# Key normalisation steps moved in VectorE's order, rho and one product on GpSimd, an earlier load of tk, and clears on GpSimd, in a decoder layer with two recurrent mixers

## The reference, cut to what matters

```python
kk = kk / jnp.maximum(jnp.linalg.norm(kk, axis=-1, keepdims=True), 1e-12)
k_mod = heads(kf * (1.0 + (a - 1.0) * rw_k_a))
# S_t = S_{t-1} diag(w_t) + (S_{t-1}(-kk_t)) (kk_t*a_t)^T + v_t k_t^T ; y_t = S_t r_t
y = _rwkv7_scan(r_h, w_h, k_mod, v_h, kk, kk * a_h)
y = (y - mu) * lax.rsqrt(var + GN_EPS) * gn_w + gn_b      # per head
y = y + jnp.sum(r_h * k_mod * rw_r_k, axis=-1, keepdims=True) * v_h
hm = _mlstm_chunkwise(mh(q2), mh(k2), mh(v2), i_pre + ml_i_b, f_pre + ml_f_b)
hm = (hm - mu) * lax.rsqrt(var + ML_NORM_EPS)             # per head
```

## Time and profile before

| what | us |
|---|---|
| median of 3 runs (lowest, highest) | 2936.3 (2933.69, 2939.88) |
| profiled execution, its own time | 2934.89 |
| its span | 2933.0 |
| TensorE busy | 2840.8 (97%) |
| VectorE, GpSimd, ScalarE busy | 1292.5, 1226.8, 581.7 |

### The profile page before, as it was taken

The page is one execution under the profiler, slowest core; times in us unless marked ns, Lnnn a source line. Parts: engine busy times, 40 slices in busy tenths (PEclk is TensorE's granted clock), DMA queues, the critical chain, the costliest instruction groups (busy, mean ns, idle before and its releaser), DMA issues.

```text
span 2933.0 us, 38258 instructions
## 1 busy us (share of the span) xinstructions
PE 2840.8 (97%) x14892; PEld 2379.6 (81%) x14892; DVE 1292.5 (44%) x1207; ACT 581.7 (20%) x908; POOL 1226.8 (42%) x651
## 2 busy tenths in 40 slices
PE   7999999999999999989999999999999999999996
PEld 5888888888888888868888888887888888888885
DVE  5331432244556524127888876532444422331344
ACT  3100110012100112125656641112311100100011
POOL 3334433443444356644556454332133443343341
PEclk9999999999999999999999999999999999999998
DMA  3111111112322234332112214320011111111112
GB/s 131 48 50 50 44 49 50 51 41 95 111 90 100 100 101 152 117 103 55 49 34 54 48 51 129 108 79 29 8 49 51 46 48 50 50 44 49 51 41 74
DMA packets 99115, 196.61 MB, mean 67 GB/s; under 512 B 14288, under 2 KB 56400, under 8 KB 98792
## 3 DMA queue, kind: packets, MB, share of 16 engines
q1 hardware_dynamic: 79072, 138.07, 16.0%
q10 hardware_dynamic: 19976, 57.59, 5.2%
HBM read 160.93 MB, written 34.67 MB: 67 GB/s over the span
## 4 chain that ended last, share of the span: by engine, by line
PE 90%; DVE 6%; issue 2%; ACT 1%; POOL 1%; DMA 1%; DVEq 0%; ACTq 0%; SPq 0%; POOLq 0%
PE G L655 26%; PE G L657 26%; PE G L656 26%; PE G L884 4%; PE G L1053 1%; PE G L787 1%; PE G L1076 1%; PE G L973 1%; PE G L781 0%; DVE ylo L1959 0%; DVE kk L1717 0%; DVE beta L1793 0%; DMA tk<-rows_d 0%; PE G L721 0%; DVE Am L1847 0%
## 5 line engine op out<-in xcount | busy, mean ns | idle before, releaser
L614 POOL TENSOR_TENSOR whi<-raw,zero 128x1024 fp32r<-128x1024 f32 (+1 forms) x213 | 398.9, 1873 | 1409.8 <-PE G L657 1406.3
L655 PE MATMUL G<-hhi,whi 128*128 128x512 f32 x2288 | 893.4, 390 | 17.8 <-DVE hlo L1538 17.8
L657 PE MATMUL G<-hhi,wlo 128*128 128x512 f32 x2288 | 890.9, 389 | 0.0
L656 PE MATMUL G<-hlo,whi 128*128 128x512 f32 x2288 | 890.9, 389 | 0.0
L617 POOL TENSOR_TENSOR wlo<-raw,whi 128x1024 fp32r<-128x1024 f32 (+1 forms) x213 | 517.3, 2428 | 16.7
L655 PEld LDWEIGHTS G<-hhi,whi 128*128 128x128 f32 x2288 | 430.0, 188 | 109.3 <-issue 15.3
L657 PEld LDWEIGHTS G<-hhi,wlo 128*128 128x128 f32 x2288 | 429.9, 188 | 89.7
L656 PEld LDWEIGHTS G<-hlo,whi 128*128 128x128 f32 x2288 | 430.1, 188 | 89.3 <-issue 0.7
L655 PE MATMUL G<-ahi,whi 128*128 128x512 f32 x960 | 374.5, 390 | 2.7 <-DVEq L436 2.7
L656 PE MATMUL G<-alo,whi 128*128 128x512 f32 x960 | 374.2, 390 | 0.0
L657 PE MATMUL G<-ahi,wlo 128*128 128x512 f32 x960 | 374.1, 390 | 0.0
(11 more groups left out here) (328 smaller groups left out, 3183.8 us busy)
## 6 DMA issues: line engine op xcount, KB each, us to landing
raw<-in_wg SPq DMA_DIRECT2D x44, 512.0 KB, 3.5
raw<-in_wu SPq DMA_DIRECT2D x44, 512.0 KB, 3.5
raw<-in_wd SPq DMA_DIRECT2D x32, 512.0 KB, 3.5
raw<-in_ml_in SPq DMA_DIRECT2D x16, 512.0 KB, 3.6
zml_d<-po ACTq DMA_DIRECT2D x16, 512.0 KB, 2.6
gates_d<-po ACTq DMA_DIRECT2D x16, 512.0 KB, 2.7
zm<-zml_d SPq DMA_DIRECT2D x8, 1024.0 KB, 5.8
sg<-gates_d ACTq DMA_DIRECT2D x16, 512.0 KB, 5.0
```

The source lines that it names most:

```text
L614: nc.gpsimd.tensor_tensor(hi, raw[:, k, 0:w], zero[:].to_broadcast([P, w]), ALU.add).then_inc(hi_made, 1)
L655: nc.tensor.matmul(dst, wh, hi, start=start, stop=False)
L656: nc.tensor.matmul(dst, wh, lo, start=False, stop=False)
L657: return nc.tensor.matmul(dst, wl, hi, start=False, stop=stop)
```

## The change

It has eight parts, all in the mixers' stage.

1. `key_root(i + 1, 0)` moves from behind level 6 to between its two updates, into the place of the product Ys*yrs. `key_root(i, 1)` moves from the end of pass i - 1 into pass i behind "cc", where `key_root(i, 2)` and `kk` go as well, ahead of gsig, ga, gu and kmod (in pass 0 they stay behind kmod).
2. The product Ys*yrs ("y1") goes from VectorE to GpSimd, as the first of its output instructions.
3. GpSimd's rho also waits for `bv` of VectorE.
4. TensorE's transposes of kap now come ahead of the mean, those of beta behind it; ScalarE copies ktok ahead of btok.
5. `tk` of segment 0 is loaded by ScalarE's queue in the projection of the gates, not by SyncE behind the barrier.
6. Am is filled in `first_keys`; Bm, Mv and Mu are cleared by GpSimd in pass 0.
7. The mLSTM's statistics (`mve`, `mmv`, lines 1889 to 1894) go from level 2 to behind the first update of level 3; `output_norm(0)` goes from level 3 to level 4.
8. FINAL_SEQ and the lists of names follow (of them the diff shows one).

```diff
--- before.py
+++ after.py
@@ -115,4 +115,4 @@
 B_ACT = ["Un", "Y0", "Y1", "lnv", "rsv"]
-B_DVE = ["dS", "S", "yc", "ve", "g1", "g2", "g3", "y1"]
-B_POOL = ["bvb", "ysq", "y2", "y3", "y4"]
+B_DVE = ["dS", "S", "yc", "ve", "g1", "g2", "g3"]
+B_POOL = ["bvb", "ysq", "y1", "y2", "y3", "y4"]
 M_PE = ["kT", "vT", "S", "num", "dC", "yT"]
@@ -481,4 +482,5 @@
                 sp.dma_start(ab[:], rows_d[0:2, :, cols].unsqueeze(0).to_broadcast([P, 2, MH, SEG])).then_inc(rows_in, 16)
-                sp.dma_start(tk[:], rows_d[2:4, :, cols].rearrange("k h t -> t k h"),
-                             allow_slow_non_contiguous=True).then_inc(rows_in, 16)
+                if back:
+                    sp.dma_start(tk[:], rows_d[2:4, :, cols].rearrange("k h t -> t k h"),
+                                 allow_slow_non_contiguous=True).then_inc(rows_in, 16)
                 sp.wait_ge(*m_dve.at("y1", i - 1))
@@ -550,3 +552,5 @@
 
-                pool.wait_ge(*b_dve.at("y1", j))
+                pool.wait_ge(*b_dve.at("g3", j))
+                tt(Ys[:], Ys[:], yrs[:], ALU.mult).then_inc(*B.sig("y1"))
+                pool.wait_ge(*B.at("y1", j))
                 tt(Ys[:], Ys[:], vbc("rw_gn_w", SEG), ALU.mult).then_inc(*B.sig("y2"))
@@ -559,2 +563,5 @@
                 tt(bvb[:], bv[:], vbc("rw_gn_b", SEG), ALU.add).then_inc(*B.sig("bvb"))
+            if front and not back:
+                for m in (Bm, Mv, Mu):
+                    nc.gpsimd.memset(m[:], 0.0)
             if front:
@@ -569,2 +576,3 @@
                 pool.wait_ge(*b_pe.at("Y", j))
+                pool.wait_ge(*f_dve.at("bv", i))
                 tt(rho[:], zs[:, 0:4, :], Pp[:, :, 1:DEC], ALU.mult).then_inc(*F.sig("rho"))
@@ -856,4 +864,2 @@
                 turn(g1[:, 1, :], zs[:, 8:12, :]).then_inc(*F.sig("vT"))
-                pe.wait_ge(*f_dve.at("bv", i))
-                turn(g0[:, 1, :], beta).then_inc(*F.sig("bT"))
                 pe.wait_ge(*f_pool.at("kap", i))
@@ -864,2 +870,4 @@
             if front:
+                pe.wait_ge(*f_dve.at("bv", i))
+                turn(g0[:, 1, :], beta).then_inc(*F.sig("bT"))
                 pe.wait_ge(*f_act.at("ktok", i))
@@ -1261,2 +1269,5 @@
                 if n == RC - 1:
+                    act.wait_ge(rows_out, 4 * 16)
+                    act.dma_start(tk[:], rows_d[2:4, :, 0:SEG].rearrange("k h t -> t k h"),
+                                  allow_slow_non_contiguous=True).then_inc(rows_in, 16)
                     act.wait_ge(x_in, 4 * 16)
@@ -1334,4 +1345,4 @@
             if front:
-                for name, dst, src in (("a", atok, g0[:, 0, :]), ("v", vtok, g1[:, 1, :]), ("b", btok, g0[:, 1, :]),
-                                       ("k", ktok, g1[:, 0, :])):
+                for name, dst, src in (("a", atok, g0[:, 0, :]), ("v", vtok, g1[:, 1, :]), ("k", ktok, g1[:, 0, :]),
+                                       ("b", btok, g0[:, 1, :])):
                     act.wait_ge(*f_pe.at(f"{name}T", i))
@@ -1720,2 +1731,3 @@
             step(nc.vector.memset(mvx[:], 1.0))
+            step(nc.vector.tensor_copy(Am[:], con(C_ID).unsqueeze(1).to_broadcast([P, NH, P])))
             key_sums(i)
@@ -1726,4 +1738,3 @@
                 dve.wait_ge(kv_out[r], (RC + RC // 2 + 1) * 16)
-            step(nc.vector.tensor_copy(Am[:], con(C_ID).unsqueeze(1).to_broadcast([P, NH, P])))
-            for m in (Bm, Mv, Mu, St, CN):
+            for m in (St, CN):
                 step(nc.vector.memset(m[:], 0.0))
@@ -1757,8 +1768,5 @@
                     tt(w, w, v, ALU.mult).then_inc(*B.sig("g2"))
-                elif k == 2:
+                else:
                     dve.wait_ge(*B.at("g2", j))
                     stt(r, w, 1.5, r, ALU.add, ALU.mult).then_inc(*B.sig("g3"))
-                else:
-                    dve.wait_ge(*B.at("g3", j))
-                    tt(flat(Ys[:]), flat(Ys[:]), r, ALU.mult).then_inc(*B.sig("y1"))
 
@@ -1775,2 +1783,5 @@
                 tt(dec[:], cum[:], hend[:].to_broadcast([P, RC, DEC]), ALU.subtract).then_inc(*F.sig("cc"))
+                if back:
+                    key_root(i, 1)
+                    key_root(i, 2)
                 dve.wait_ge(*l_act.at("gt", i))
@@ -1785,4 +1796,5 @@
                     ALU.mult).then_inc(*F.sig("kmod"))
-                for k in range(2 if back else 0, 3):
-                    key_root(i, k)
+                if not back:
+                    for k in range(3):
+                        key_root(i, k)
                 dve.wait_ge(*n_dve.at("kk", i))
@@ -1816,5 +1828,7 @@
                 output_variance()
-                for k in range(4):
+                for k in range(3):
                     output_norm(k)
                 return
+            if back:
+                dve.wait_ge(*B.at("S", j))
             tt(pend[:], Pp[:, :, DEC - 1:DEC], con(C_ONES, 1).unsqueeze(1).to_broadcast([P, RC, 1]),
@@ -1862,3 +1876,11 @@
                         nc.vector.bn_stats(mst[:, h, :], hm[:, h, :])
-                if n == 3 and back:
+                if n == 3:
+                    dve.wait_ge(*M.at("st", i))
+                    nc.vector.memset(mve[:], 0.0)
+                    for h in range(MH):
+                        last = nc.vector.bn_aggr(mmv[:, h, :], mst[:, h, :])
+                    last.then_inc(*M.sig("mv"))
+                    dve.wait_ge(*M.at("mv", i))
+                    ts(mve[:], mmv[:, :, 1], ML_EPS, None, ALU.add).then_inc(*M.sig("ve"))
+                if n == 4 and back:
                     output_norm(0)
@@ -1866,4 +1888,4 @@
                     output_norm(1)
-                if n == 6 and back:
-                    output_norm(3)
+                if n == 6 and more:
+                    key_root(i + 1, 0)
                 update(n, 1)
@@ -1887,9 +1909,2 @@
                     tt(CN4, CN4, pairs_of(G[3]), ALU.add).then_inc(*M.sig("C"))
-                    dve.wait_ge(*M.at("st", i))
-                    nc.vector.memset(mve[:], 0.0)
-                    for h in range(MH):
-                        last = nc.vector.bn_aggr(mmv[:, h, :], mst[:, h, :])
-                    last.then_inc(*M.sig("mv"))
-                    dve.wait_ge(*M.at("mv", i))
-                    ts(mve[:], mmv[:, :, 1], ML_EPS, None, ALU.add).then_inc(*M.sig("ve"))
                 if n == 3:
@@ -1915,4 +1930,2 @@
                     gram("Mv", Mv, G[3], C_UPEQ)
-            if more:
-                key_root(i + 1, 0)
             dve.wait_ge(*f_pe.at("F", i))
@@ -1922,6 +1935,3 @@
             dve.wait_ge(*f_pe.at("B", i))
-            if more:
-                key_root(i + 1, 1)
-            else:
-                nc.vector.memset(mnw[:], 0.0)
+            nc.vector.memset(mnw[:], 0.0)
             gram("B", Bm, G[3], C_UP)
```

More of the change, by code:

```diff
@@ L103 @@
 LATE = {5: ["Mu"], 6: ["Mv"]}
-F_PE = (["bonus", "aT", "vT", "bT", "kT", "A"] + [f"A0{x}" for x in SETS]
+F_PE = (["bonus", "aT", "vT", "kT", "bT", "A"] + [f"A0{x}" for x in SETS]
         + [y for n in range(1, LEVELS) for y in [f"W{n}a", f"V{n}a", f"W{n}b", f"V{n}b", f"E{n}a"] + LATE.get(n, [])
@@ L107 @@
         + ["F", "V", "B", "UQ", "gate", "Wst", "Z"])
-F_ACT = (["P", "Pi", "atok", "vtok", "btok", "ktok"] + [f"Ar{x}" for x in SETS]
+F_ACT = (["P", "Pi", "atok", "vtok", "ktok", "btok"] + [f"Ar{x}" for x in SETS]
          + [f"{y}{n}{x}" for n in range(1, LEVELS) for x in SETS for y in ("Wc", "Tc")] + ["Tc", "W1c", "gev", "Zc"])
@@ L125 @@
 XO_PE, XO_ACT, XO_DVE = ["T", "O"], ["pt0", "pt1", "hi"], ["lo"]
-ROWS_SEQ, ROWS_ACT, FINAL_SEQ = 15, 3, 53
+ROWS_SEQ, ROWS_ACT, FINAL_SEQ = 15, 3, 50
 ROWS_END = ROWS_SEQ + 17
@@ L263, in layer_kernel @@
     dec, idr = mix("dec", (P, RC, DEC)), mix("idr", (P, RC * P), F32R)
+    tk = mix("tk", (P, 2, MH))
     assert top["mix"] <= po_at
@@ L267, in layer_kernel @@
     AL = mix("AL", (P, 2, NH, SEG), F32R)
-    ab, tk = mix("ab", (P, 2, MH, SEG)), mix("tk", (P, 2, MH))
+    ab = mix("ab", (P, 2, MH, SEG))
     nmt, aden, mve, mrs, mnw = (mix(n, (P, MH)) for n in ("nmt", "aden", "mve", "mrs", "mnw"))
```

## The result

The changed kernel takes 2951.9 us in the median of five runs (2941.5 to 2953.2), the kernel before 2936.3, which is a median of five runs too, not of three: ratio 1.0042, 95% interval 1.0022 to 1.0062. I had predicted 2921.2. The sign is wrong, although the middle of the stage does what the prediction says. Two of the five took 2941.5 and 2944.6 us and three 2952 to 2953, and the profile is of the one at 2941.5, so it lacks what the upper group adds (see rho_back).

A forecast was written before the change was run, and what follows sets the result against it. TensorE, busy 50.32 of 52.87 us a pass, bounds the kernel, so only its idle time can go. 6 x 1.8 + 1.1 + 3.6 - 0.4 = 15.1 us off 2934.89 gives 2919.8; the median, 1.4 higher, 2921.2; range 2914 to 2930.5.

The forecast's parts named there:

- Parts 5 and 6, the start: In pass 0, tk's earlier load and fewer clears and copies start the levels 3.6 us sooner.
- 6 x 1.8: Six passes, the last included, each 1.8 us shorter.
- The upper gain: Largest gain allowed: 2.1 us a pass, 1.4 + 4.6 at the start, given as 18.3 us, time 2918.
- Parts 1a to 1c and 4: In a pass, VectorE's results come sooner for TensorE and ScalarE is ready 1.76 us sooner: 1.8 us gained.
- The three waits: TensorE's waits on VectorE for St (0.93 us), Uf (0.67) and bv (0.33), 1.93 us a pass, all go.
- Parts 2, 3 and 7 at nothing: Ys*yrs on GpSimd, rho's wait and the moved statistics cost nothing; bounds -0.15 and +0.4 us a pass.
- my bound of 0.4: The upper bound on what Ys*yrs on GpSimd, rho's wait and the moved statistics cost: +0.4 us a pass.
- The rule on the lock: VectorE with two SBUF inputs and a reading GpSimd instruction lock each other, later blocks; Uf about 0.5 us later.
- First transition: From pass 0 to 1, dec already waits for ScalarE and comes no sooner: only 1.1 us gained.
- GpSimd decides and the kernel is slower: GpSimd's queue from Ys*yrs to ab holds up S0s, Uf and kmod: +5.9 us or more, 2942 us; chance 4%.

The follow-up runs named there:

- rho_back: The changed kernel without rho's wait for bv on GpSimd: 2952.1 us.
- tk_back: The changed kernel with tk at its old place in memory and loaded on SP's queue behind ab, as before: 2922.3 us, ratio 0.9951.
- keys_only: The kernel before with only the key steps moved (step 0 into level 6, steps 1 and 2 ahead of gsig): 2922.8 us, ratio 0.9947.
- pad: The changed kernel with 64 unused bytes behind tk, so AL lies 128 bytes from its first place, tk still loaded early: 2934.3 us, ratio 0.9991.
- again: The changed kernel, no edit, profiled and timed a second time: 2947.4 us.
- awake: The changed kernel with 19 unread matmuls of 512 columns on TensorE ahead of dC in the last pass: 2930.4 us.
- nudge: The changed kernel with two 4-wide memsets on VectorE ahead of aden in the last pass: 2942.5 us.
- delay: The changed kernel with one 512-wide memset on VectorE ahead of aden in the last pass: 2945.2 us.
- y1_back: The changed kernel with the product Ys*yrs on VectorE again, in level 6: 2946.1 us.
- stats_back: The changed kernel with the mLSTM statistics in level 2 again: 3006.4 us.
- shift: keys_only with tk allocated ahead of Ur, moving Ur, Tr, Wr, Qr, AL and ab by 64 bytes, no instruction moved: 3005.4 us, ratio 1.0235.
- only_al: keys_only with 64 unused bytes ahead of AL and tk behind mmv, so only AL and ab move by 64 bytes: 3007.0 us.
- stall: The kernel before, with TensorE's dC in the last pass also waiting for GpSimd's zm, put off by two memsets: 2956.4 us, ratio 1.0063.
- pad_look: The same kernel as pad, run again for one more profile: 2926.2 us.
- pad_stats: The kernel pad with the mLSTM statistics in level 2 again: 2924.2 us.
- calm: The changed kernel, where in the last pass GpSimd waits for hm ahead of its masks of level 3: 2932.5 us, ratio 0.9976.
- best: pad_stats, with GpSimd also waiting for hm ahead of its masks of level 3 in the last pass: 2917.5 us, ratio 0.9927.

## Why the prediction was wrong

- *Parts 5 and 6, the start: the step that failed.* I counted tk's load, the clears and the copies, and nothing for the tile's new place, which moves AL by 64 bytes. No rival had it. With the old place and the old load of tk the time is 25 to 30 us lower (tk_back 2922.3 against 2951.9 and 2947.4); in keys_only the place alone costs 83. The kernel pad keeps the early load and moves AL on: its two profiled executions took 2922.7 and 2922.2 us, the changed kernel's first 2941.5, and the prediction's sum for a profiled execution was 2919.8. So 19 of the 22 us by which it is off come with AL's place, and 3 with the other terms.
- *What is shown of the place.* aden of the last pass lasts 5.24 to 5.88 us in all ten traces with AL 64 bytes on and GpSimd's row unbroken (after, again, awake, nudge, delay, rho_back, y1_back, stats_back, shift, only_al), and 1.22 to 1.24 us in all seven with AL in its first place or 128 bytes on (before, stall, keys_only, tk_back, pad, pad_look, pad_stats). only_al moves no instruction and, of the tiles that the masks touch, AL alone. Not settled: why the masks are some 15 ns longer there, whether that length or the place itself makes the difference, by what rule GpSimd keeps VectorE out, and what happens in the slower half of pad's executions. pad moves the small tiles nmt to mmv by 64 bytes as well. Other places than these three were not tried.
- *The sum, "6 x 1.8".* It took the last pass for a pass like the others. It lost 19.1 us, and even with a harmless place of AL it gains 0.5 (pad and tk_back), not 1.8. There GpSimd has no kk and ksq between its masks of levels 2 and 3, so aden meets a mask; in the middle passes it meets ksq and comes through at its end, although masks follow without a gap. The earlier trace rows are of that pass; I read them for Uf alone. (The upper gain is 18.2 us by its own terms, not 18.3.)
- *The clock.* The prediction prices waits at their length and has no term for the clock. In calm, again and stall a wait of 1.15 to 5.2 us cost 10 to 20.
- *Parts 1a to 1c and 4.* The three waits went as said. 1.8 a pass is right as a total (1.79), but by two errors that cancel. From TensorE's gate product (L964, now L972) to ScalarE's first copy of level 1 it is 23.12 us before and 20.90 after, so 2.2 sooner and not 1.76. keys_only, without part 4, has 20.91, so part 4 gave nothing there. Without the statistics in level 3 a pass gains 2.5 in all (pad_stats), and their new order takes 0.6 of it back.
- *Parts 2, 3 and 7 at nothing.* Right for y1 and rho (y1_back and rho_back leave the pass at 51.1). Wrong for the statistics, outside my bound of 0.4: mve takes 1.02 us ahead of an update for which TensorE waits.
- *The rule on the lock.* I weighed the rule that the prediction cites for y1 and the keys, and took "the later one blocks" for a wait for one instruction. It fits in that VectorE is held only while GpSimd works (aden 0.16 us in calm); but aden was held behind five instructions that GpSimd began after it.
- *First transition and start.* 2.6 gained instead of 1.1. A's cut in pass 0 stands 21.4 us after TensorE's first matmul behind the barrier (24.2 before): 2.8 instead of 3.6, and the wait in level 3 with its low clock then gives back more than that (Uf of pass 0 at 1364.07, before 1363.18). In tk_back, with the old load of tk, the whole of pass 0 gains 0.7.
- *The rival "GpSimd decides and the kernel is slower"* named the right engine and the wrong place and mechanism, with 4%.

## What to carry to other kernels

Treat an allocation line in a diff as a change of its own: measure it alone, or keep the hot tiles in their places. Look at the first and last pass for an unbroken row on GpSimd, and keep small VectorE instructions on which TensorE waits out of its reach, or break the row with a wait, as in best. Price each new wait of TensorE by what the clock does after it, not by its length.
